# A hybrid decoder step on one core: TensorE's rounds over the RWKV pairs without a loop, and chunk products on four quarters of the array

## The reference

```
def step(S, inp):                       # rwkv7_scan, for each of 16 heads of 64
    rt, wt, kt, vt, at, bt = inp
    sa = einsum('bhij,bhj->bhi', S, at)
    S = S * wt + sa[..., None] * bt + vt[..., None] * kt
    return S, einsum('bhij,bhj->bhi', S, rt)
```

## Time and profile before

| | us |
|---|---|
| median of 3 runs | 4871.41 |
| lowest and highest run | 4868.46, 4887.18 |
| the profiled execution's own time | 4880.07 |
| its span, first to last instruction | 4878.2 |
| PE busy | 4206.2 |
| DVE busy | 1656.4 |
| ACT busy | 1195.4 |
| the eight rounds, from the first inverse to the last `states` | 790.5 |

### The profile page before, as it was taken

How to read it: one execution, slowest core, us unless ns; L and a number is a source line. 1 busy time by engine, 2 the same in 40 slices (tenths; PEclk the granted TensorE clock), 3 DMA queues, 4 the chain that set the end, 5 groups by cost and what they waited for, 6 DMA issues and landing times.

```text
span 4878.2 us, 84875 instructions
## 1 busy us (share of the span) xinstructions
PE 4206.2 (86%) x35567; PEld 3739.9 (77%) x35567; DVE 1656.4 (34%) x1948; ACT 1195.4 (25%) x1610; POOL 345.7 (7%) x502
## 2 busy tenths in 40 slices
PE   7879788797769999996879978888887799999967
PEld 4656666556659999996849967777776699999957
DVE  2413414225243223234252234444442432232332
ACT  2111212212132112123112224444342321121132
POOL 1110110201100000000030000101100000000000
PEclk9979979799789999998989989999898899999989
DMA  2211111201201111110012210000101011111111
GB/s 74 62 53 31 54 40 49 62 10 38 72 26 44 40 48 43 45 44 26 27 37 81 81 62 22 23 22 25 36 9 34 26 44 44 44 46 41 40 31 58
DMA packets 305311, 206.39 MB, mean 42 GB/s; under 512 B 26281, under 2 KB 290143, under 8 KB 304927
## 3 DMA queue, kind: packets, MB, share of 16 engines
q1 hardware_dynamic: 290174, 161.38, 11.3%
q0 software_dynamic: 11200, 25.97, 2.0%
q10 hardware_dynamic: 3552, 13.41, 0.7%
HBM read 173.66 MB, written 27.04 MB: 41 GB/s over the span
## 4 chain that ended last, share of the span: by engine, by line
issue 48%; PE 27%; DVE 7%; PEld 6%; ACT 4%; POOLq 3%; ACTq 1%; DVEq 1%; PEldq 1%; POOL 1%; DMA 0%; SPq 0%
PE ps L1535 25%; PEld ps L1535 6%; ACT big L611 2%; DVE big L1002 2%; POOLq L281 1%; DVE big L1092 1%; POOLq L511 1%; ACT L611 1%; PE ps L1929 1%; POOL big L283 1%; ACTq L703 1%; DVE big L1325 1%; DVE h_hi L1002 1%; POOLq L283 0%; DVE wparts L1002 0%
## 5 line engine op out<-in xcount | busy, mean ns | idle before, releaser
L1535 PE MATMUL ps<-h_hi,wparts 128*128 128x364 f32 (+1 forms) x4992 | 1010.5, 334 | 73.2 <-DVEq L1185 55.2
L1535 PEld LDWEIGHTS ps<-h_hi,wparts 128*128 128x128 f32 x4992 | 867.6, 191 | 78.0 <-DVEq L1185 59.8
L1535 PE MATMUL ps<-x_lo,wparts 128*128 128x364 f32 (+1 forms) x3360 | 698.0, 332 | 42.9 <-DVE h_hi L1002 42.9
L1535 PE MATMUL ps<-x_hi,wparts 128*128 128x364 f32 (+1 forms) x3072 | 599.6, 330 | 60.0 <-DVEq L1185 53.4
L1535 PE MATMUL ps<-big 64*64 64x64 f32 (+6 forms) x6744 | 531.3, 270 | 129.3 <-ACTq L703 43.8
L1535 PEld LDWEIGHTS ps<-x_lo,wparts 128*128 128x128 f32 x3360 | 581.5, 190 | 48.1 <-issue 36.0
L1535 PEld LDWEIGHTS ps<-big 64*64 64x64 f32 (+3 forms) x6744 | 434.1, 164 | 185.6 <-issue 60.3
L1535 PEld LDWEIGHTS ps<-x_hi,wparts 128*128 128x128 f32 x3072 | 524.5, 189 | 61.9 <-DVEq L1185 53.7
L611 ACT ACTIVATE big<-ps 128x512 f32<-128x512 f32 (+13 forms) x306 | 194.2, 660 | 1452.8 <-PE ps L1535 447.9
L1535 PE MATMUL ps<-h_lo,wparts 128*128 128x364 f32 (+1 forms) x2112 | 472.8, 333 | 0.0
L611 ACT ACTIVATE wparts<-ring 128x1024 fp32r<-128x1024 f32 x200 | 198.3, 1001 | 780.7 <-PE ps L1535 768.3
(11 more groups left out here) (215 smaller groups left out, 3703.9 us busy)
## 6 DMA issues: line engine op xcount, KB each, us to landing
ring<-in_mlp_up SPq DMA_DIRECT2D x64, 512.0 KB, 4.0
ring<-in_mlp_down SPq DMA_DIRECT2D x64, 512.0 KB, 3.7
ring<-in_w_in_even SPq DMA_DIRECT2D x28, 512.0 KB, 6.9
rkv_scratch<-big ACTq DMA_DIRECT2D x24, 544.0 KB, 2.7
big<-rkv_scratch SPq DMA_DIRECT2D x24, 544.0 KB, 5.2
big<-in_cache_k SPq DMA_DIRECT2D x128, 64.0 KB, 1.9
big<-in_cache_k POOLq DMA_DIRECT2D x128, 64.0 KB, 2.1
big<-in_cache_v SPq DMA_DIRECT2D x128, 64.0 KB, 1.9
```

The costliest lines, as they stand in the source:

```text
L1535: return pe.matmul(out, lhsT, rhs, start=start, stop=stop, skip_group_check=True)
```

## The change

PE's loop over the first seven pairs is written out: the same `inverse`, `states` and `chunks` seven times with constants in place of the register. The other four engines keep their loops. `hold` becomes a plain wait. In the dense block of `states`, in `y_part` and in steps 1 and 2 of `beside_scan` the two column halves h are no longer done one after the other; each block b goes round the quarters (h, q) = (0, 0), (1, 1), (0, 1), (1, 0). The number of matmuls, their shapes and the places where a step signals stay as they were; steps 1 and 2 and steps 4 to 7 now each do a share of the blocks for both heads instead of one head's.

```diff
@@ -1827,10 +1827,8 @@
                 used = job("rout", 0, q)[1]
                 pe.wait_ge(job_free[q], used + 1)
             pe.wait_ge(rw_masks, 1)
-            def hold(semaphore, value):
-
-                pe.wait_ge(semaphore, value)
-                pe.sem_inc(passed, 1)
+            hold = pe.wait_ge
+            tiles = ((0, 0), (1, 1), (0, 1), (1, 0))
 
             def mm64(out, r, lhsT, rhs, start=True):
 
@@ -1906,7 +1904,7 @@
             def gram(blk):
 
                 for m in range(2):
-                    for h, q in ((0, 0), (1, 1), (0, 1), (1, 0)):
+                    for h, q in tiles:
                         c, at = blk * P + q * CH, blk % 2 * 256 + m * P
                         last = mm64(out64(2 * h + blk // 2 % 2, at, 64 * q, P).rearrange("p (r t) -> p r t", r=2),
                                     64 * h, bks[m][:, c:c + CH], ar2[:, :, c:c + CH])
@@ -2053,11 +2051,11 @@
                         lora_w(n)
                     grow(i, lv, 1)
 
-            def y_part(h, b):
-
-                for q in range(2):
+            def y_part(b):
+
+                for h, q in tiles:
                     mm64(out64(2 + q, b * CH, 64 * h), 64 * q, hc("VTK", h, b), at_(h, b, 3), b == 0)
-                for q in range(2):
+                for h, q in tiles:
                     mm64(out64(2 + q, b * CH, 64 * h), 64 * q, at_(h, b, 2), at_(h, b, 1), False)
 
             def y_state(c):
@@ -2070,9 +2068,9 @@
             def beside_scan(i, n, c):
 
                 if c <= 2:
-                    for b in range(BLKS):
-                        for q in range(2):
-                            last = mm64(out64(2 + q, b * CH, 64 * (c - 1)), 64 * q, at_(c - 1, b, 0), at_(c - 1, b, 1))
+                    for b in range(4 * c - 4, 4 * c):
+                        for h, q in tiles:
+                            last = mm64(out64(2 + q, b * CH, 64 * h), 64 * q, at_(h, b, 0), at_(h, b, 1))
                     if c == 2:
                         last.then_inc(mhq_done, 1)
                 elif c == 3:
@@ -2087,8 +2085,8 @@
                 elif c <= 7:
                     if c == 4:
                         hold(mhq_ok, i * 4 + 2)
-                    for g in range(4):
-                        y_part((c - 4) // 2, (c - 4) % 2 * 4 + g)
+                    for b in range(2 * c - 8, 2 * c - 6):
+                        y_part(b)
                 elif c == 8:
                     for r in (0, 64):
                         mm64(out64(5, 0, r, 512), r, xs_("KTK"), w["VM"])
@@ -2141,17 +2139,15 @@
                 if n is not None:
                     bonus(n)
                 hold(tu_ok, i * 3 + 3)
-                for h in range(2):
-                    for b in range(BLKS):
-                        for q in range(2):
-                            last = mm64(out64(2 + q, b * CH, 64 * h), 64 * q, at_(h, b, 0), hc("BTK", h, b))
+                for b in range(BLKS):
+                    for h, q in tiles:
+                        last = mm64(out64(2 + q, b * CH, 64 * h), 64 * q, at_(h, b, 0), hc("BTK", h, b))
                 last.then_inc(mhq_done, 1)
-                for h in range(2):
-                    for b in range(BLKS):
-                        for q in range(2):
-                            mm64(out64(q, b * CH, 64 * h), 64 * q, hc("KTK", h, b), hc("VTK", h, b), b == 0)
-                        for q in range(2):
-                            last = mm64(out64(q, b * CH, 64 * h), 64 * q, hc("BTK", h, b), at_(h, b, 2), False)
+                for b in range(BLKS):
+                    for h, q in tiles:
+                        mm64(out64(q, b * CH, 64 * h), 64 * q, hc("KTK", h, b), hc("VTK", h, b), b == 0)
+                    for h, q in tiles:
+                        last = mm64(out64(q, b * CH, 64 * h), 64 * q, hc("BTK", h, b), at_(h, b, 2), False)
                 last.then_inc(mhq_done, 1)
                 hold(mhq_ok, i * 4 + 1)
                 for c in range(1, NCH):
@@ -2173,7 +2169,7 @@
             pe.wait_ge(rw_dve, 5)
             bonus(0)
             chunks(0)
-            with pe.Fori(0, KT - 1) as i:
+            for i in range(KT - 1):
                 inverse(i, i + 1)
                 states(i, i + 1)
                 chunks(i + 1, i)
```

## The result

| | before | after |
|---|---|---|
| median of the timed runs, us | 4877.86 (4868.46 to 4887.18) | 4801.59 (4799.37 to 4807.95) |
| the profiled execution, its span | 4880.07, 4878.2 | 4807.95, 4806.1 |
| first inverse to the end of the last `states` | 786.2 | 699.9 |
| from there to the end | 1183.5 | 1195.6 |

The ratio is 0.9844, with an interval of 0.9822 to 0.9866: 76 us less, where 40 were forecast. In the two profiled executions the difference is 72.1 us: the rounds give 86.3, the part ahead of them costs 2.1 more and the part behind them 12.1 more. (The 2.1 say nothing: where the code ahead of the rounds is the same, it took 2900 to 2911 us in the traces.) So two things are to be explained: a gain in the rounds of twice the size forecast, and a loss in code that the change doesn't touch.

What follows compares the result with a forecast made beforehand. PE was taken as the bound: its own matmuls in dense stretches, a PE, ACT, PE chain in the scan, plus idle loop edges. 24.8 + 15.2 = 40 us off the median 4871.4 gave 4831 us, range 4806 to 4850.

Steps and rivals of the forecast that it cites:

- part 1: PE's loop edges between rounds: writing out the loop removes idle time before the inverse, 24.8 us, bounds 20 to 27.
- Part 2: PE's `hold` as a plain wait: 0.1 us less where really waited for, nothing where already satisfied.
- part 3: Dense block and scan: four quarters at 14.6 ns a record; with the scan's `hold`s 1.9 us a round.
- rival 2: In the rounds: instruction supply is no limit and the stall at step 12 goes too; about 4813 us, chance 0.15.
- Rivals 3 and 4: Clock halves in the scan, 4895 us, chance 0.06; branch time returns as stalls in straight code, 4865, chance 0.03.

## Why the prediction was wrong

Of the 40 us forecast, 24.8 were part 1 and 15.2 parts 2 and 3. In the traces the loop took 34.8 us off the rounds, the waits and the quarters 51.5.

**Part 1 held at the edges and was too small.** 24.8 us were forecast there; `chunks` and edge lost 24.7 in the kernel with the loop alone, whose time fell by 30. But the rounds fell by 34.8, over the upper bound of 27: most of the other 10 lie in the inverse and the states 8 to 15. With the loop went the arithmetic on registers ahead of the waits in it too, 280 instructions of 32 or 37 ns; whether that gave the 10 us, no run shows.

**Part 2 is the step that failed.** "0.1 us less where the wait is really waited for, nothing where it is already satisfied": some 3 us were counted, beside what part 3 had of it. Measured in straight code, plain waits took 30.4 us off the rounds. The row that would have told me was on the table: the stall on "issue" at step 12 of the scan. I read it, and that of the earlier trace rows, as the supply of instructions at its limit, 62 a us, and so as a bound on part 3. It was a late packet, but no limit of the supply: with plain waits and the old order the same matmuls, in 1.4% fewer instructions, ran with 0.5 us of such idle time. I never asked what could make the supply late; that `hold` could was no part of the sum. The stall's end was put into rival 2, at 5 to 8 us; the states 8 to 15 lost 17.1 us in all, since the half clock behind it and the `hold`s' own time go too.

**Part 3 was mis-sized, the mechanism was right.** Block, first state and states 0 to 8 together took 114.9 us before and 87.0 after, 27.9 less; the upper bound for this stretch was 3.0 a round, 24. Of that 4.9 came with the loop and the waits, so the quarters gave 23.0 or 2.9 us a round, against 1.9 (with the `hold`s of the scan in it) taken as a middle between 0.4 and 3.4. The block's 14.6 ns a record, DVE as the one that is late next, and 0.74 us a step were each as forecast. The middle was not the mean of a spread: where no stall falls into the block the upper end is reached, where one does, about 1.2 us is lost again. The sixth round shows it:

```profile
3416.02 2.77 PE L1535 MATMUL ps<-big 64*64 64x64 f32 x170
3420.01 0.57 PE L1535 MATMUL ps<-big 64*64 64x64 f32 x22 [1.21 <-issue]
```

So at this density a packet still comes too late in three of eight rounds; that is 2.7 of the 5.4 us on "issue" that are left. By the Trainium skill's sentence on instruction fetch ("Runtime: NRT & Kernel Launch", Instruction fetch mechanics) the passage from block to block is mostly hidden. That holds with plain waits and two quarters (0.5 us on "issue"), not with `hold` (14.3 us).

**Two parts of one change were priced as if they were independent.** The quarters alone, in the loop with `hold`, gave a ratio of 0.9996; behind the plain waits they gave 21 us of the rounds in the traces and 30 us of the medians.

**What was left out.** That the six further copies of a round move all of PE's code behind them was not considered. It costs 12 us in the trace, in a loop that was not in the diff, and some 13 us in the medians, by the runs with 40 increments. It also hid a part of the error: without it the time would lie still further below the forecast.

The rounds, in the traces: 34.8 us by the loop, 30.4 by the waits, 21.1 by the quarters, 86.3 in all; less 12.1 behind them and 2.1 ahead of them, 72.1. Rival 2, at 4813, came nearest. Rivals 3 and 4 did not occur: the clock stands at 1.00 in states 0 to 8 of all eight rounds of the changed kernel (the line is that of the third), and the jumps' time did not come back as stalls, for "issue" fell from 46.1 to 14.3 us with the loop alone.

```profile
3142.90:3150.64 7.74, 6.06 (x234) 4.82 (x236) 7.25 (x8) 2.52 (x9) 0.00 (x0) 1.00 0.02 4
```

## What to carry to other kernels

An idle time on "issue" in straight code can be an instruction packet that came late without being a limit of the supply: see when the packets come, look for waits that are instructions of their own before it, and make them plain waits. Price the parts of a change together where one feeds the other; quarters that run twice as fast are worth little if the stream behind them stands. When code is written out, look at every loop behind it, whose head has moved, and try a few useless instructions, or write that loop out as well.

## What the runs showed of the hardware

A loop's head at a bad place cost each trip of 193 us some 2.7 us of idle time and 3.4 us at half clock (in the trip shown), and a third instruction packet where there were two; 40 instructions ahead of the loop cured it, 256 brought it back. A far jump back on PE takes its sequencer 3.4 to 3.9 us in the median of a loop, of which 1 us showed at an MLP trip's edge and 3.9 at a head's. On four quarters 192 records of 64x64x64 take 3.03 us in any of three orders, about 15 ns each. A stall on "issue" of 0.6 to 2 us in the rounds ended 1.2 to 1.6 us after an instruction packet of 16 KB, 112 times of 112.
